# Heads and cross products of a state group spread between two halves of the B projection, and one early modulation block on VectorE

## What is computed

```python
shift, scale, gate = adaln(c, ada_w[0], ada_b[0])      # silu(c) @ ada_w + ada_b, 3 x 2048
h = modulate(rms_norm(x, norm_g[0]), shift, scale)     # the same with c_ctx for the context
p = h @ w_in                                           # q, gate, z, k, v, x, B, C, dt
# neighbourhood attention over q, k, v, and beside it for each of 8 groups of 4 heads:
cb = einsum('bign,bjgn->bijg', C, B)
w = cb * decay * dt                                    # one 256 x 256 matrix per head
y = w @ x_head + (C @ state) * exp(cs)                 # within the sequence, and across from the context
y = y + d * x_head
yb = rmsnorm(y * silu(z)) * g                          # per group
```

## Time and profile before

| | us |
|---|---|
| median of three runs | 3008.98 (3008.62 to 3011.77) |
| the profiled execution, its time | 3011.94 |
| its span in the profile | 3010.0 |
| PE busy | 2929.5 (97%) |
| DVE busy | 766.1 (25%) |
| ACT busy | 392.0 (13%) |
| POOL busy | 48.4 (2%) |

### The profile page before, as it was taken

How to read it: one execution, slowest core, us unless ns; L and a number is a source line. 1 busy time by engine, 2 the same in 40 slices (tenths; PEclk the granted TensorE clock), 3 DMA queues, 4 the chain that set the end, 5 groups by cost and what they waited for, 6 DMA issues and landing times. The chain is left out here.

```text
span 3010.0 us, 30148 instructions
## 1 busy us (share of the span) xinstructions
PE 2929.5 (97%) x12192; PEld 2221.4 (74%) x12192; DVE 766.1 (25%) x1515; ACT 392.0 (13%) x761; POOL 48.4 (2%) x68
## 2 busy tenths in 40 slices
PE   7999999999999999999999999999999999999999
PEld 1267876677666555555658888888888888888888
DVE  1252333243332244444443001001010100001110
ACT  0121101111110122222211001000000011111110
POOL 0010000000000000000000000000000000000000
PEclk9999999999999999999999999999999999999999
DMA  8874555465461333332224454555554444444432
GB/s 349 283 249 145 186 183 171 147 203 191 145 183 53 99 98 98 98 92 80 82 95 148 147 167 140 158 150 152 155 152 155 138 141 140 122 134 141 146 124 72
DMA packets 379149, 444.85 MB, mean 148 GB/s; under 512 B 20308, under 2 KB 351560, under 8 KB 378312
## 3 DMA queue, kind: packets, MB, share of 16 engines
q1 hardware_dynamic: 353200, 361.15, 39.4%
q0 software_dynamic: 17408, 67.11, 6.5%
q10 hardware_dynamic: 8472, 15.58, 1.4%
HBM read 439.56 MB, written 4.26 MB: 147 GB/s over the span
## 5 line engine op out<-in xcount | busy, mean ns | idle before, releaser
L458 PE MATMUL bank<-hT,w 128*128 128x256 f32 (+1 forms) x6144 | 1635.9, 428 | 6.0 <-ACT hT L998 4.5
L458 PEld LDWEIGHTS bank<-hT,w 128*128 128x128 f32 x6144 | 1176.1, 192 | 438.5 <-issue 311.4
L458 PE MATMUL bank<-w,hT 128*128 128x256 f32 (+1 forms) x2176 | 461.7, 373 | 0.0
L458 PEld LDWEIGHTS bank<-w,hT 128*128 128x128 f32 x2176 | 403.0, 190 | 59.8 <-issue 8.1
L458 PE MATMUL bank<-yT,w 128*128 128x256 f32 x2048 | 445.1, 379 | 1.4 <-DVE yT L1674 1.0
L458 PEld LDWEIGHTS bank<-yT,w 128*128 128x128 f32 x2048 | 388.2, 190 | 54.3 <-DVE yT L1674 1.2
L998 ACT ACTIVATE work<-bank 128x512 f32<-128x512 f32 (+3 forms) x292 | 153.7, 556 | 1721.7 <-PE bank L458 1716.7
L1505 DVE SCALAR_TENSOR_TENSOR work<-xT,silc,work 128x512 f32<-128x512 f32 x240 | 180.5, 752 | 39.6 <-DMA xT<-in_ada_w 31.7
L998 ACT ACTIVATE work<-work 128x512 f32<-128x512 f32 (+4 forms) x243 | 135.0, 556 | 195.0 <-DVE work L1571 128.1
L458 PE MATMUL bank<-work 128*128 128x256 f32 (+2 forms) x400 | 117.5, 415 | 15.6 <-ACT work L998 11.3
L458 PEld LDWEIGHTS bank<-work 128*128 128x128 f32 x400 | 74.7, 196 | 39.9 <-ACT work L998 15.1
(11 more groups left out here) (107 smaller groups left out, 839.4 us busy)
## 6 DMA issues: line engine op xcount, KB each, us to landing
w<-in_na_ssd_w_in SPq DMA_DIRECT2D x48, 2048.0 KB, 8.3
xT<-in_ada_w POOLq DMA_DIRECT2D x64, 1024.0 KB, 5.6
w<-in_sc_w_in SPq DMA_DIRECT2D x32, 2048.0 KB, 10.6
w<-in_w_in SPq DMA_DIRECT2D x32, 2048.0 KB, 10.6
w<-in_ada_w SPq DMA_DIRECT2D x16, 2048.0 KB, 10.4
w<-in_na_ssd_w_out SPq DMA_DIRECT2D x16, 2048.0 KB, 8.8
w<-in_na_ssd_w_in SPq DMA_DIRECT2D x16, 1024.0 KB, 7.4
w<-in_sc_w_out SPq DMA_DIRECT2D x8, 2048.0 KB, 8.3
```

Of the source, the lines that this page charges most:

```text
L458: return nc.tensor.matmul(dst, lhsT, rhs, start=start, stop=stop, skip_group_check=free)
```

## The change

In the early stage one of the four blocks, columns 3072 to 4095, leaves PE. Its four loads go through w[3], issued by POOL, and DVE multiplies each of 16 row chunks by its factor and accumulates into eacc, 128x1024 for each of the two conditions (`early_part`). PE sums eacc over the partitions by 16 products against ones. The other three blocks use three slots, 12 loads. The transposes of x all stand behind the sixth load's products, and their copies are shared: even chunks on DVE, odd on ACT. The norm's sum and product move behind the blocks.

In the state stage the weights' order on DVE stays. On PE, head 0 stands directly behind the state products; half of B's projection follows, then head 1, the cross products and head 2, then the other half of B, and head 3 ahead of C. On ACT, `conv_in(g, 2)` stands ahead of `ssd_rms`. The last group, behind the loop, keeps its order.

```diff
+    eacc = L(2, 4 * TILE)
...
+        for t in range(4):
+            wait(gp, early_taken, t)
+            gp.dma_start(w3.rearrange("p (a b) -> p a b", a=4), w_ada[0][:, 4 * t:4 * t + 4, 12 * TILE:16 * TILE]).then_inc(
+                early_in, 16)
...
-        for b in range(EARLY):
-            for q in range(SLOTS):
-                wait(sp, ada_used, (b - 1) * SLOTS + q + 1)
-                sp.dma_start(early(q), w_ada[0][:, 4 * q:4 * q + 4, b * 4 * TILE:(b + 1) * 4 * TILE]).then_inc(
-                    w_loaded[q], 16)
-        sp.wait_ge(xt_dve, DC)
+        for u in range(12):
+            wait(sp, ada_used, u - 2)
+            sp.dma_start(early(u % 3), w_ada[0][:, 4 * (u % 4):4 * (u % 4) + 4, (u // 4) * 4 * TILE:(u // 4 + 1) * 4 * TILE]
+                         ).then_inc(w_loaded[u % 3], 16)
+        sp.wait_ge(xt_dve, DC // 2)
+        sp.wait_ge(xt_act, DC // 2)
...
-                    return sp.wait_ge(ada_used, (EARLY - 1) * SLOTS + s + 1)
+                    return sp.wait_ge(ada_used, 10 + s) if s < 3 else sp.wait_ge(early_taken, 4)
...
+            if s == 3:
+                extra -= 16 * EARLY
...
-        def featured(dst, s, ch, width, ready=None):
-
-            for kc in range(DC):
+        def featured(dst, s, ch, width, ready=None, chunks=range(DC)):
+
+            for kc in chunks:
...
-            wait(pe, xt_dve, kc - 1)
+            wait(pe, xt_dve if kc % 2 == 0 else xt_act, kc // 2)
...
+        for u in range(12):
+            b, q, s = u // 4, u % 4, u % 3
+            if q == 0:
+                wait(pe, ada_row, 2 * (b - 1))
+            pe.wait_ge(w_loaded[s], 16 * (u // 3 + 1))
+            tile = w[s][:, :, :].rearrange("p a b -> p (a b)").rearrange("p (a b) -> p a b", a=4)
+            for kc in range(4):
+                for half in range(2):
+                    last = mm(rows_of[half][0:2, :], pair[:, 4 * q + kc, :],
+                              tile[:, kc, half * 512:(half + 1) * 512], q + kc == 0, q + kc == 6)
+            last.then_inc(ada_used, 1)
+            if u == 5:
+                for kc in range(DC):
+                    x_turned(kc)
+            if u == 6:
+                early_turn(0)
+            if u == 10:
+                early_turn(1)
+        pe.wait_ge(cols_dve, 2)
+        norm_sums(0, T + TC)
+        pe.wait_ge(early_taken, 4)
+        for ch in range(8):
+            for k in range(2):
+                n = 64 + 4 * ch + 2 * k
+                last = mm(bank[0][:, n:n + 2], eacc[:, k, ch * P:(ch + 1) * P], ONES[:, 0:2])
+        last.then_inc(ada_turned, 1)
+        early_turn(2)
...
-                ssd_apply(s)
+                ssd_within(s, 0)
             loaded(1, "ssd", g)
             dst = accumulate("ssd", 2, g)
-            featured(dst[:, :], 1, 0, T + TC).then_inc(acc_full, 1)
+            featured(dst[:, :], 1, 0, T + TC, None, range(DC // 2))
+            if not first:
+                ssd_within(s, 1)
+                ssd_across(s)
+                ssd_within(s, 2)
+            featured(dst[:, :], 1, 0, T + TC, None, range(DC // 2, DC)).then_inc(acc_full, 1)
+            if not first:
+                ssd_within(s, 3)
             dst = accumulate("ssd", 3, g)
             featured(dst[:, 0:T], 1, 1, T).then_inc(acc_full, 1)
             loaded(2, "ssd", g)
@@ -734,23 +755,31 @@
                 pe.wait_ge(acc_free, BANKS["out"] + cb - 1)
             out_half(cb, ch, 0)
 
-        def ssd_apply(s, beside=None):
+        def ssd_apply(s, beside):
+            ssd_across(s)
+            for r in range(4):
+                if r == 2:
+                    beside()
+                ssd_within(s, r)
+
+        def ssd_across(s):
             pe.wait_ge(s_h, s + 1)
             pe.wait_ge(s_xtk, s + 1)
             for ib, dst in enumerate((bank[5][:, :], wide[:, 0:512])):
                 last = mm(dst, cmT[:, ib * P:(ib + 1) * P], hst)
             last.then_inc(s_ys, 1)
-            wait(pe, s_yz, 1 * s)
-            for r in range(4):
-                if beside and r == 2:
-                    beside()
-                pe.wait_ge(s_wm, 4 * s + r + 1)
-                for ib in range(2):
-                    o = ib * TILE + r * 64
-                    for jb in range(2):
-                        last = mm(bank[4][:, o:o + 64], wm[:, r % 2, jb * T + ib * P:jb * T + (ib + 1) * P],
-                                  xtk[:, jb, r * 64:(r + 1) * 64], jb == 0, jb == 1)
-                last.then_inc(s_yi, 1)
+
+        def ssd_within(s, r):
+            if r == 0:
+                pe.wait_ge(s_xtk, s + 1)
+                wait(pe, s_yz, 1 * s)
+            pe.wait_ge(s_wm, 4 * s + r + 1)
+            for ib in range(2):
+                o = ib * TILE + r * 64
+                for jb in range(2):
+                    last = mm(bank[4][:, o:o + 64], wm[:, r % 2, jb * T + ib * P:jb * T + (ib + 1) * P],
+                              xtk[:, jb, r * 64:(r + 1) * 64], jb == 0, jb == 1)
+            last.then_inc(s_yi, 1)
...
-            act.wait_ge(xt_dve, DC)
+            for kc in range(1, DC, 2):
+                act.wait_ge(xt_pe, kc + 1)
+                A(xT[:, kc, :], bank[5][:, 0:T], ACT.Copy)
+                A(cxT[:, kc, :], bank[5][:, T:2 * T], ACT.Copy).then_inc(xt_act, 1)
+            act.wait_ge(xt_act, DC // 2)
+            act.wait_ge(xt_dve, DC // 2)
...
+            conv_in(g, 2)
             if not first:
                 ssd_rms(g - 1)
-            conv_in(g, 2)
...
+        def early_part(q):
+            dve.wait_ge(early_in, 16 * (q + 1))
+            tile = w3.rearrange("p (a b) -> p a b", a=4)
+            for kc in range(4):
+                for k in range(2):
+                    s = sil[:, 16 * k + 4 * q + kc:16 * k + 4 * q + kc + 1]
+                    if q + kc == 0:
+                        last = v.tensor_scalar(eacc[:, k, :], tile[:, kc, :], s, None, ALU.mult)
+                    else:
+                        last = v.scalar_tensor_tensor(out=eacc[:, k, :], in0=tile[:, kc, :], scalar=s, in1=eacc[:, k, :],
+                                                      op0=ALU.mult, op1=ALU.add)
+                if kc < 3:
+                    link(last)
+            last.then_inc(early_taken, 1)
+            dve.wait_ge(early_taken, q + 1)
+
+        early_part(0)
         early_rows(0)
-        for kc in range(DC):
+        early_part(1)
+        for kc in range(0, DC, 2):
             dve.wait_ge(xt_pe, kc + 1)
-            turned = bank[1 if kc % 2 == 0 else 5]
-            v.tensor_copy(xT[:, kc, :], turned[:, 0:T])
-            v.tensor_copy(cxT[:, kc, :], turned[:, T:2 * T]).then_inc(xt_dve, 1)
+            v.tensor_copy(xT[:, kc, :], bank[1][:, 0:T])
+            v.tensor_copy(cxT[:, kc, :], bank[1][:, T:2 * T]).then_inc(xt_dve, 1)
         dve.wait_ge(cols_pe, 2)
         v.tensor_copy(colp[:, P:4 * P], bank[2][:, P:4 * P]).then_inc(cols_dve, 1)
+        early_part(2)
         early_rows(1)
         norm_sum_squares(0, 2, T + TC)
+        early_part(3)
         early_rows(2)
-        early_rows(3)
...
-        v.tensor_tensor(mod[:, 0, 0:32, :], bank[0][:, 0:64].rearrange("p (a b) -> p a b", b=2), bias,
+        v.tensor_tensor(mod[:, 0, 24:32, :], bank[0][:, 64:96].rearrange("p (a b d) -> p a b d", b=2, d=2)[:, :, :, 0:1].rearrange("p a b d -> p a (b d)"),
+                        bias[:, 24:32, :], ALU.add)
+        v.tensor_tensor(mod[:, 0, 0:24, :], bank[0][:, 0:48].rearrange("p (a b) -> p a b", b=2), bias[:, 0:24, :],
                         ALU.add).then_inc(mod_ready, 1)
```

## The result

| | before | changed |
|---|---|---|
| median, us | 3010.14 (3008.62 to 3011.77, 4 runs) | 2941.42 (2939.39 to 2945.16, 4 runs) |
| span of the profiled execution | 3010.0 | 2936.8 |
| mean granted clock | 0.985 | 0.993 |

The ratio is 0.9773, 95% interval 0.9756 to 0.979: 68.7 us faster, 67 forecast. The profiled execution of the changed kernel is the fastest of its four (2939.39) and that of before (3011.94) lies 1.8 us above its median, so the spans differ by 73.2 us, not 68.7.

The account below looks back on a forecast made before the run. PE was taken to bound the kernel. State stage -49 and early stage -18 sum to -67 us, counted from the median of 3009.0 to 2942 us; range 2932 to 2964, with rivals 1 to 3 taken in for the most part.

Parts of the forecast that it names:

- Stretch without waits 27.64 us: State stage, PE from state products to z: cost without waits at 2.4 GHz, leaving 51.2 us as all that could go.
- The clock stays up: State stage, PE: no clock fall in the reordered stretches; if it fell as before, at most 24 us lost.
- No wait is left; the z bank is the nearest limit, slack 0.7 us: State stage: PE's waits go; the second z bank is freed after 13.1 us, and PE wants it at 13.8.
- Rival 2: State stage: z bank becomes the new wait; 3 us delay costs 2.3 a group, +16, 2958 us; chance 0.09.
- Rival 4: State stage: large z bank wait before z's second half, the chain being 25 us long, 3020 us; chance 0.03.
- The convolution's own wait of 5.16 us: State stage, DVE's wait for the B copy: goes only because ACT copies ahead of the rms, else some 4 us later.
- Rival 5: State stage: reorder only moves the wait for weights to head 3; -18 alone, 2991 us; chance 0.02.
- The early term: Early stage: one block moved off PE, less its costs, gives -18 us, bounds -26 and -8.
- first loads: Early stage: POOL's load shares the DMA engines, PE starts 0 to 7.5 us late, gets 2.0 back; +4 us.
- x transposes in one stretch: Early stage, PE: sixteen transposes together take about 11.6 us against 11 in four stretches; +1 us.
- clock behind them: Early stage, PE: the longer transpose stretch precedes a clock fall; +1.5 us (0 to 3.4).
- waiting for DVE: End of early stage: DVE's chain of 47.2 us ties with PE's 46.6; +1 us (0 to +3).

Follow-up runs that it names:

- e5: The changed kernel with B not split: state products, heads 0 and 1, cross products, B whole, heads 2 and 3, C; 2941.62 us.
- e4: The changed kernel with all of a group ahead of B: state products, head 0, cross products, heads 1 to 3, then B whole; 2969.89 us.
- e11: The changed kernel with four more DVE operations on 128x512 at the end of combine, some 2.9 us a group; 2963.55 us.
- e3: The changed kernel with ACT's copy of B (conv_in 2) back behind the rms, as before the change; 2940.16 us.
- e9: The changed kernel with DVE's third part ahead of the parameter transposes' wait and POOL's first load issued after w[0] landed; 2937.61 us.

## Why the prediction was right

The time (2942 against 2941.4) and both terms held: state -49 against -51.1, early -18 against -19.4. By its steps:

- *Stretch without waits 27.64 us.* Measured 27.66, seven times. I took 0.3 us a group off for joints between shapes; there is none, and the whole 51.2 us of the sum came.
- *The clock stays up.* It did, in all seven. The split of B is not what keeps it up (e5 has none), and with 2.2 us of waits left in a group it fell again in five of seven (e4).
- *No wait is left; the z bank is the nearest limit, slack 0.7 us.* The slack was 0.9, and e11 turned 2.9 us of added DVE work into waits of 2.0. Rival 2's condition did not come, and its price was too low: I had 2.3 us a group for 3 us of delay, 16 in all, from the waits alone. e11's waits were of that size, but with the clock that fell behind them 2.9 us of delay cost 22. Rival 4 has the same mechanism and would have needed 10 us more on the chain.
- *"The convolution's own wait of 5.16 us ... goes only because that copy now stands ahead of the rms."* Wrong, by e3. I compared the copy with B's end and not with the moment when DVE is free to use it, 6.6 us after head 3; behind the rms it is there at 5.9. The old wait of 5.16 us went because B itself ends sooner against the combine: before, B was projected behind all heads. The step carried nothing of the sum.
- *Rival 5, head 3's weights.* They come 2.4 us after head 1 and PE wants them 9.5 us after it, as counted.

The early term came to nearly the right sum by luck, from errors that cancel:

| step | predicted | measured |
|---|---|---|
| 64 records less | -27.6 | -27.6 |
| products against ones, one turn less | +1.9 | +2.4 (48 records 6.11, before 32 in 3.73) |
| first loads | +4 | +6.8 (first block's end 46.4, now 53.2) |
| x transposes in one stretch | +1 | +0.6 (11.62 against 4 x 2.76) |
| clock behind them | +1.5 | -1.4 (the next block at full pace; before 29.07) |
| waiting for DVE | +1 | 0 |

The measured column sums to -19.2, where the attention stage's first product came 19.4 us sooner. Two terms are off by 2.8 to 2.9 us, one each way: the first loads and the clock. The start was late by only 1.4 us (15.92, where I had written 18 to 20), but the wait before the second load grew from 2.0 to 5.35, where I had let it vanish, and 1.8 more went because the clock fell in that wait (22.56 us for 48 records, before 20.76). I shared the DMA engines for w[0] only, not for the load behind it. DVE's term was too high since I scaled the 752 ns of L1505; that operation does not double with its columns, 1.25 us at 1024. From DVE's last x copy to the end of its fourth part it took 44.8 us, not 47.2; PE needed it after 46.2 (I had 46.6).

The clock's term had the wrong sign. I had put the fall at 87.2 us down to the transposes. The windows of the changed kernel's transposes, of the products behind them, and of the fall that came instead:

```profile
66.82:78.44 11.62, 8.66 (x65) 6.84 (x65) 5.62 (x15) 4.62 (x14) 0.00 (x0) 1.00 0.91 362
78.44:85.40 6.96, 6.96 (x17) 1.28 (x17) 0.43 (x2) 6.82 (x4) 0.00 (x0) 1.00 0.00 1
27.40:34.20 6.80, 3.60 (x5) 0.60 (x6) 5.77 (x5) 0.00 (x0) 0.65 (x1) 0.50 1.03 389
```

64 transpose records in 11.6 us, a quarter of it waits of 0.4 to 0.5 us, kept the full clock. The Trainium skill's page "TensorE: Matmul & The Clock Gate" (Part 4) has transposes not count as activity; this trace does not agree. What stood ahead of the fall at 87.2 before was a short run of transposes and then sixteen records of 2x2; which of the two did it, no run singled out. What I drew from the page "SBUF — State Buffer" (the SWDGE box), a late third part, did not come: POOL issued it at 64.8 us, 2.8 us ahead of DVE's first x copy (67.58) and not at the copies, and it took 11.4 us to land, the shortest of the four:

```profile
L332 POOL DMA_DIRECT2D w<-in_ada_w x1: 742/742/742, 64.8 to 64.8; - x1
...
DMA to landing us min/median/max: 11.4/11.4/11.4
```

The issue was over before the first copy began. Those copies also read PSUM, and the page speaks of copies within SBUF. So this trace does not test its rule.

## What to carry to other kernels

Where a producer with two buffers feeds an engine in order, don't let the first two products stand behind an unrelated wait: put what is ready first, and fill with independent work of at least one production time between product n and product n + 2. Price such a reorder by the stretch without waits at the full clock, start to start of rows, not by the idle time alone: here 25.8 us idle carried some 24 more of slow clock (half of seven falls of 6.8 us). And before an edit is called necessary, compare the time at which its result is there with the time at which the consumer is free, not with the time at which its input is ready.

## What I had not expected of the hardware

- Short waits bring the clock down even between full products: in e11, 2.0 us of waiting and then 3.4 us at 1.2 GHz; in e4, 0.7 and 1.5 us of waiting within 9.1 us of short records. Not each time: six groups of e11 waited 2.0 us, and it fell in four; in e4 it fell in the five that had waited 0.73 or 0.74 and 1.48, but not in one that had waited 1.03 and 1.48, nor in one with a single wait of 1.37.
- 5.3 us of state products, two heads and cross products (256, 64 and 512 columns) without a wait (e5), and 11.6 us of transposes with seven waits of 0.4 to 0.5 us, did not.
- Until the x transposes the DMA engines are full (413 to 416 GB/s from 5 to 25 us in the kernels before, changed and e9; 405 from 25 to 50 and 383 from 50 to 66 in the changed one), and no order of the first loads tried took more than 3 us from the stage's end.
